# Two weight loads for the next leg, asked for behind the query products or behind the sixteen best pairs

## The reference, cut to what matters

```
h = rms_norm(x, norm1_g) * (1 + sc1) + sh1
u_a, u_b, v_b, q, ckv, qi, ki, wi = split(h @ w_in)            # 1732 columns
mix = concat(ssm_mixer(u_a), gmlp_mixer(u_b, v_b), dsa_mixer(q, ckv, qi, ki, wi))
x = x + g1 * (mix @ w_out)
h = rms_norm(x, norm2_g) * (1 + sc2) + sh2
x = x + g2 * peer_ffn(h)
```

```
q = h @ w_q                                    # 8 heads x 2 halves x 64
v1, i1 = top_k(q_half0 @ sub_k1.T, 16);  v2, i2 = top_k(q_half1 @ sub_k2.T, 16)
top_s, pos = top_k(v1[:, None] + v2[None, :], 16)        # the sixteen best pairs
gates = softmax(top_s)
act = gelu(einsum(peer_u[experts], h));  out = einsum(gates * act, peer_v[experts])
```

## Time and profile before

| what | value |
|---|---|
| median of 3 runs | 3650.46 us |
| the profiled execution: its time | 3636.02 us |
| its span | 3634.2 us |
| granted TensorE clock, mean | 0.692 of full speed |
| VectorE busy | 2227.8 us, 61% |
| GpSimd busy | 2283.0 us, 63% |
| TensorE busy (matmul) | 1836.1 us, 51% |
| moved by DMA | 1282.62 MB, mean 353 GB/s |

### The profile page before, as it was taken

One profiled execution on the slowest core, in us unless ns is written; L12 is line 12 of the kernel. 1 busy time (PEld: TensorE's weight loads), 2 busy tenths in 40 slices (PEclk: granted clock), 3 DMA queues, 4 the chain that ended last, 5 costly groups with the idle time before them and its releaser, 6 DMA issues.

```text
span 3634.2 us, 30323 instructions
## 1 busy us (share of the span) xinstructions
PE 1836.1 (51%) x10176; PEld 894.3 (25%) x10176; DVE 2227.8 (61%) x5807; ACT 250.6 (7%) x683; POOL 2283.0 (63%) x2067
## 2 busy tenths in 40 slices
PE   6825452736454562566636455465636465233333
PEld 4425230513132230231304122232304122000000
DVE  6267757675768557765486746676585856645420
ACT  1200100001000100101000010001000110000000
POOL 0015667677667667555666766777676776767653
PEclk9767575767677776776758677676857676555666
DMA  6547899999999999999999999999999999999996
GB/s 247 211 158 267 302 409 342 357 369 390 379 352 368 337 406 364 407 415 405 382 375 374 349 360 396 343 378 361 398 370 366 358 370 412 361 362 378 361 344 232
DMA packets 314671, 1282.62 MB, mean 353 GB/s; under 512 B 34955, under 2 KB 35211, under 8 KB 303507
## 3 DMA queue, kind: packets, MB, share of 16 engines
q0 software_dynamic: 294912, 1073.87, 78.2%
q1 hardware_dynamic: 18740, 201.83, 13.7%
q10 hardware_dynamic: 864, 4.99, 0.4%
HBM read 1272.16 MB, written 8.39 MB: 352 GB/s over the span
## 4 chain that ended last, share of the span: by engine, by line
POOL 31%; PE 18%; DVE 16%; DMA 16%; issue 14%; another core or an unknown queue 5%; ACT 1%; SPq 0%; POOLq 0%; DVEq 0%; ACTq 0%
POOL ringV L236 18%; POOL ringU L226 13%; DMA ringV<-in_peer_v,idxP 9%; PE py L479 6%; DVE ringU L803 5%; DMA ringU<-in_peer_u,idx_g 5%; PE pj L551 4%; DMA ringU<-in_peer_u,idx_w 2%; PE pj L718 1%; PE pj L622 1%; PE pj L494 1%; PE pj L558 1%; PE pw L692 1%; PE pw L519 1%
## 5 line engine op out<-in xcount | busy, mean ns | idle before, releaser
L803 DVE CUSTOM_DVE_ANT_0 ringU<-ringU,h2g 128x1024 f32<-128x1024 f32 x1024 | 1224.6, 1225 | 800.0 <-DMA ringU<-in_peer_u,idx_g 549.7
L236 POOL DMA_INDIRECT ringV<-in_peer_v,idxP x1024 | 1144.6, 1118 | 581.4 <-issue 272.3
L479 PE MATMUL py<-ringV,wm 128*32 128x512 f32 x4096 | 817.8, 914 | 1125.2 <-DMA ringV<-in_peer_v,idxP 924.8
L226 POOL DMA_INDIRECT ringU<-in_peer_u,idx_g x960 | 1071.4, 1116 | 472.1 <-issue 284.2
L479 PEld LDWEIGHTS py<-ringV,wm 128*32 128x32 f32 x4096 | 160.3, 145 | 1646.9 <-issue 1575.9
L551 PE MATMUL pj<-hT,wring 128*128 128x128 f32 (+1 forms) x2560 | 329.8, 292 | 26.7 <-issue 18.8
L551 PEld LDWEIGHTS pj<-hT,wring 128*128 128x128 f32 (+1 forms) x2560 | 317.4, 201 | 63.3 <-issue 50.7
L226 POOL DMA_INDIRECT ringU<-in_peer_u,idx_w x64 | 62.2, 971 | 269.4 <-DVE gate_w L1299 246.1
L692 PE MATMUL pw<-hT,ckv_all 128*128 128x128 f32 x320 | 78.9, 401 | 94.1 <-issue 60.7
L718 PE MATMUL pj<-wring,mixT 128*128 128x512 f32 x256 | 118.3, 622 | 9.1 <-issue 8.4
L494 PE MATMUL pj<-ident,wk 128*128 128x128 f32 x168 | 43.5, 364 | 138.6 <-DVE wk L1165 61.3
(11 more groups left out here) (294 smaller groups left out, 1893.0 us busy)
## 6 DMA issues: line engine op xcount, KB each, us to landing
wring<-in_w_in SPq DMA_DIRECT2D x28, 2048.0 KB
wring<-in_w_mod SPq DMA_DIRECT2D x24, 2048.0 KB
wring<-in_w_out SPq DMA_DIRECT2D x16, 2048.0 KB
wring<-in_peer_w_q SPq DMA_DIRECT2D x16, 2048.0 KB
ringV<-in_peer_v,idxP POOLq DMA_INDIRECT x1024
ringU<-in_peer_u,idx_g POOLq DMA_INDIRECT x960
wring<-in_w_in SPq DMA_DIRECT2D x8, 784.0 KB
x_mix<-xs SPq DMA_DIRECT2D x8, 512.0 KB
```

The lines of the kernel that those rows point to most:

```text
L226: pool.indirect_dma_start(out=ringU[k % NR][:, :], out_offset=None, in_=ux, in_offset=bass.IndirectOffsetOnAxis(ap=idx[:, k:k + 1], axis=0 ...
L236: pool.indirect_dma_start(out=ringV[r % NR][:, :], out_offset=None, in_=vx, in_offset=bass.IndirectOffsetOnAxis(ap=idx[:, at:at + 1], axis=0),
L479: mm = t.matmul(py[32 * j:32 * j + 32, c * 512:(c + 1) * 512], wm[e % 2][:, at:at + 32], ringV[(4 * m + j) % NR][:, c * 512:(c + 1) * 512] ...
L803: v.tensor_tensor_reduce(out=ringU[k % NR][:, :], in0=ringU[k % NR][:, :], in1=h2g[:, :], scale=1.0, scalar=0.0, op0=ALU.mult, op1=ALU.add ...
```

## The change

One wait is added to SyncE's program, ahead of the two loads for the next leg. It is there in the eight legs with mixers.

```diff
@@ -1399,6 +1399,7 @@
                         weights(A["peer_w_q"][l], c0, 512)
                     sp.wait_ge(S["x1_ready"], 2)
                     sp.dma_start(x_mix[bass.ds(b * T, T), :], xs[:, :]).then_inc(S["x1_saved"], 16)
+                    sp.wait_ge(S["top_ready"], 1)
                     for c0, width in GROUPS[:2]:
                         weights(A["w_in"][l], c0, width)
                 if not mixers:
```

## The result

The changed kernel takes 3702.6 us (median, 3697.3 to 3720.0) against 3649.2 of the kernel before on the same chip: a ratio of 1.0149, 95% interval 1.0117 to 1.0182. It is slower by 53 us. The prediction was 3629 (3600 to 3670) and is wrong in its sign. The profiled execution took 3719.97 us, 17 us more than the median, so its stages overstate the loss; the second profile of it, `e12_changed_again`, is used beside it.

A forecast was written before the change was run, and what follows sets the result against it. The prediction took the gathers of U and V rows to bound the kernel. Six legs at 8.5 - 6.2 us, leg 4 at 8.5 - 1 and leg 0 at 0 gave 21 us less: 3629 us, range 3600 to 3670.

The forecast's parts named there:

- What bounds the kernel: Whole span: gathers of U and V rows bound it; from the loads' old place to `top_ready` DMA engines are always busy.
- The wait itself: On SyncE, some 90 us long in most legs, holding up nobody but the leg's end: cost 0.
- What it removes: 4.19 MB leave the full stretch before `top_ready` in legs 1 to 7: 8.5 us won a leg, bounds 4 and 10.3.
- What it adds: Loads behind `top_ready` delay the last V rows: 6.2 us in six legs, 1 in leg 4, 0 in leg 0.
- a room of 1.7 MB: From `top_ready` to the last mixing, at 398 GB/s, 1.7 of the loads' 4.19 MB fit without delay.
- The next leg's start: The last V fetches and first eight U fetches shift with the last mixing and not more: 0 beyond the 6.2 us.
- The sum: Whole kernel: six legs at 2.3 us, 13.8, leg 4 at 7.5, leg 0 at 0: together 21 us less.
- D: Rival: the load starves the gather rings behind `top_ready`, only 5 to 6 us won in front: 3671 us, chance 0.25.
- C: Rival: win 7 and delay 7 a leg, only leg 4 wins: 3643 to 3657 us, chance 0.20.
- B: Rival: the full 10 us won in front, delay only 4 at the leg's end: 3605 us, chance 0.13.
- What would show it: Profile test: `top_ready` 8 to 10 us sooner, last stretch about 6 longer; wrong if under 6 sooner or over 9 longer.

The follow-up runs named there:

- e12_changed_again: The changed kernel unaltered, run and profiled again on another chip, against the kernel before: 3693.6 us, 1.0166.
- e1: The kernel before with the two loads for the next leg left out: 3627.5 us, 1.0017 of the kernel before.
- f1: The kernel before with the two loads left out, repeated on another chip: 3649.9 us, 0.9998 of the kernel before.
- f3: The changed kernel unaltered, on the same chip as the second run without loads: 3695.8 us, 1.0094 of the kernel before.
- e3: The kernel before, loads kept at the old place and the same pair loaded again behind `top_ready`: 3672.2 us, 1.0139.
- e6: The kernel before plus both loads again behind `top_ready`, each cut into four DMAs with 4 KB rows instead of 16: 3623.7 us, 1.0155.
- e5: The kernel before plus only the first of the two loads again behind `top_ready`: 3591.1 us, 1.0072.
- e4: The kernel before with the added wait in legs 0 and 4 alone: 3626.1 us, 1.0011.
- e2: The kernel before with the loads waiting for the key scores (`s_ps`) instead of `top_ready`: 3615.4 us, 0.9993.
- e9: The kernel before with VectorE's dots in the first top-16 taken in finer helpings, loads at the old place: 3559.9 us, 0.9983.
- f4: The changed kernel with finer helpings of dots in the first top-16: 3663.5 us.
- f2: The kernel before with finer helpings of dots in the first top-16 and the two loads left out: 3615.1 us, 0.9899.

## Why the prediction was wrong, step by step

**What bounds the kernel.** The gathers, and the bandwidth they get: right as a mean. The DMA engines are busy for the whole time from the old place of the loads to `top_ready`, as I wrote. Wrong was to take from it that every byte less shortens it; I read that off one window of 93.5 us at 388 GB/s. Without the loads some 20 us of it run at 258 to 325 GB/s (e1, f1), and only the loads made them look full. The trace of before could have told it: GpSimd's U fetch that waits 5.78 us for a dot in the middle of a stretch called full.

**The wait itself, cost 0**: right. Nothing but the loads is behind it, and leg 0 ends at 253.09 against 253.08.

**What it removes, 8.5 us a leg (bounds 4 and 10.3)**: this is the step that failed. It is 0 (e1 1.0017, f1 0.9998), outside my bounds. Two readings of waits were behind it. The earlier trace rows is leg 1, the largest of the seven: between the first load and the scores TensorE's mixing waited for V rows 7.85 us in leg 1, 2.04 in leg 5, 4.92 in leg 6, 5.52 in leg 7, and not at all in legs 2, 3 and 4. That is 20.3 us, where the sum has 59.5. And VectorE's 14.86 us did go (its longest wait for U rows there is 5.45 in leg 1 of e1), but VectorE came no sooner to its top-16: it waited for the scores instead. Its idle time ahead of the first top-16 over the whole span, before, in e1 and in f1:

```profile
L1207 DVE MAX8 pr<-pw 128x8 f32<-128x128 f32 x128 | 26.3, 279 | 34.5 <-PE pw L733 33.7 <-DVE pr L1219 0.7
...
L1207 DVE MAX8 pr<-pw 128x8 f32<-128x128 f32 x128 | 26.3, 282 | 72.8 <-PE pw L733 65.4 <-remote 7.4
...
L1207 DVE MAX8 pr<-pw 128x8 f32<-128x128 f32 x128 | 26.3, 280 | 70.9 <-PE pw L733 54.0 <-remote 16.9
```

So 36 to 38 us of waiting for rows turned into waiting for TensorE's scores, which came no sooner behind the `x_mix` store, and the rows that landed sooner filled the rings ahead of the hole, in which they are made good. In the sum, 7 x 8.5 = 59.5 us of gain are missing. The prediction named this for its lower bound ("if the rest turns into another wait") and then gave it half a wait, where nothing was right. Why TensorE is no faster with its V rows there is in part open: "issue" gaps between its instructions stand where the wait was.

**What it adds, 6.2 us in six legs and 1 in leg 4**: right in size, in part by luck. 6 x 6.2 + 1 = 38 us; the stretches behind `top_ready` grew by 42 us from f1 to f3 and by 26 and 39 from before to the two profiles of the changed kernel, and e3 and e6 have 46 and 48. The rate was 358 to 371 GB/s in legs 1 and 2 and not the 398 I took. With 367 (leg 2) the same working gives room for 1.0 MB and a delay of 8.7 us, more than the 3.7 to 6.0 us a leg that the stretch grew in the changed kernel, so a rate taken too high made up for a delay that the working had too strict; why it is shorter is open. That the cost goes by bytes, whatever the rows' length, e5 and e6 bear out. They do not bear out a room of 1.7 MB: by that, e5 (2.1 MB) would have cost 1 us a leg, and it cost 26 us. For leg 4, e4 shows no cost that can be told from the forecast 1 us; in the first profile that stretch is 27.4 us against 24.6.

**The next leg's start at 0**: right, as far as the traces tell. The first column of the first table is 21 to 35 us longer with late loads, but in e3 and e6, which have the same late pair, it is as long as in e2 and e9 on their chips (1876 and 1879, 1831 and 1828), and with finer helpings it is 1875 with the late pair (f4) and 1889 without (f2). What lengthens it in the three profiles of the changed kernel is open.

**The sum.** With the front at 0, the forecast's own terms give 38 us more, 3636.0 + 38 = 3674, or 3689 at the median of the runs. Measured are 53 us (1.49%), 60 (1.66%) and on the chip of the f set 34 (0.94%). What makes the first two larger than 38 is not accounted for.

**The rivals.** D had the side and the condition (the delay at the end larger than the win in front), but gave the front 5.5 us as well and so stopped at 3671. Its 9.5 us a leg at the end is above the 3.7 to 6.0 of the traces. Its mechanism, rings starved by the load's share of the engines, is not what e6 shows: shares changed, the price did not. The Trainium skill, "DMA: Bandwidth & Descriptors", section "Queues, rings and completion order", which I had beside it, says that an engine takes turns between its queues by packets. The traces agree, with 79.4% for the load of long rows and 47.0% for that of short rows in e6, but it doesn't decide the cost. The Trainium skill, "DMA: Bandwidth & Descriptors", section "Specifications", has about 358 GB/s of HBM for one core. The trace still disagrees: 405 GB/s over 20 us in leg 3 above. Still, the rate of 358 to 371 at the leg's end, where loads and gathers were both queued, was nearer to it than to my 398. C, the wash, and B fall by the verdict.

**What would show it.** The test that I had written down was right: the stretch to `top_ready` had to get shorter by 6 us or more a leg, "then something else than bandwidth held it", and it did not. The last stretch grew by 3.7 us a leg in the first profile (26 / 7), 5.6 in e12 (39 / 7) and 6.0 from f1 to f3 (42 / 7), under the 9 of D.

## What to carry to other kernels

Before a transfer is moved away from a busy stretch, look at the DMA rate in steps of a microsecond, for the time behind it too: what it displaces may land in a hole that comes later, and then it costs nothing where it is. The cheapest test is to leave it out; if that wins nothing, no other place can, on that chip. Read a wait in every leg before multiplying it by their number, and ask what its end would wait for next. Two rings fed by one in-order issuer are coupled, so a long block of the engine that empties one also stops the other. Cutting the block finer won 1.0% here where no load filled the hole, and nothing that could be told from noise where one did (0.9983 [0.9959, 1.0006]). Compare on one chip: the same pair of kernels, finer helpings with late loads and without loads, differed by 2.6% across two chips and by 1.16% on one.

## What the runs showed of the hardware

The stretches that are full hold 377 to 434 GB/s in steps of 0.5 us with gathered 4 KB rows alone (the two views of leg 3, the first from 3.5 us on). Beside a load of 16 KB rows the single steps scatter (164 to 631 in the first 3.5 us), with a mean of 428 GB/s over 10 us.

GpSimd takes 0.94 us for an indirect DMA of 128 rows and 0.30 before the next; beside some stretches of VectorE's work 1.68 to 1.99 us. With 0.30 that is 128 rows of 4 KB in 1.24 us, or 423 GB/s, and in 2.29 us 229 GB/s, an estimate from these rows: beside such VectorE work the issuing alone is under the rate at which such rows land. Which VectorE operations do this was not tried.

VectorE started on the scores 8.3 to 11.7 us behind the end of TensorE's last score product in five of the eighteen legs of the changed kernel's three profiles (the two-part leg 4 not counted), and 0.0 to 1.9 us behind it in the others. In the leg shown the profile puts its wait down to "remote", and TensorE's next instructions have "issue" gaps in the same time (4.88 us before 1354.87). The cause is open.
